# Expert 0's rows gathered by TensorE with a one-hot matrix, the other experts' rows by DMA

## The chip, the cores and the metric

The kernel runs on one core of a Trainium2 chip. The metric is the device time of one launch in microseconds, lower is better. The core has a matrix engine (TensorE, PE in the rows), VectorE (DVE), ScalarE (ACT), GpSimd (POOL) and SyncE (SP), an on-chip memory of 128 partitions (SBUF), the matmul output memory of eight banks (PSUM), and 16 DMA engines to the memory off chip (DRAM).

## The reference, cut to what matters

One decoder layer over 512 tokens of width 1024: input projections, block-sparse attention and a gated recurrence, an output projection and a layer norm. The result of this norm, x1, goes through a mixture of 16 experts, two for each token, and a second norm:

```
x = layer_norm(DEEPNORM_ALPHA * x + mix, ln1_g[l], ln1_b[l])          # x1
g_w, g_idx = lax.top_k(softmax(xt @ w_group + b_group), 1)            # one group of four
e_w, e_idx = lax.top_k(e_prob, EXPERT_TOPK)                           # two experts in it
for e in range(N_EXPERTS):
    h = jax.nn.silu(xt @ w_gate[e]) * (xt @ w_up[e])
    y = y + combine[:, e:e + 1] * (h @ w_down[e])
x = layer_norm(DEEPNORM_ALPHA * x + moe, ln2_g[l], ln2_b[l])
```

## The kernel before

The kernel is written out for each engine, with semaphores between them. No planner orders the work: each engine runs its own list from top to bottom.

Products in float32 are done in three passes. A matrix is split into a high part, which ScalarE copies in a rounded form (`hi`, `ehi`, `xt_hi`), and a low part, which VectorE gets by subtraction (`lo`, `elo`, `xt_lo`). The helper `three` (lines 537 to 541) then issues three matmuls. Weights come in units of 1 MB, which SP loads into a ring of 12 slots. The split writes them into 3 working buffers, and TensorE multiplies from there.

After the output projection x1 lies in SBUF as `x_res`, token by token, in ring slots 9 and 10; the norm's weights are in slot 11. SP writes x1 to DRAM (line 384), and TensorE transposes it for the router's logits. VectorE chooses the experts (lines 1472 to 1511). TensorE counts the tokens ahead of each token in its expert, and VectorE makes from this `r_at1`, each token's place in its expert.

For each expert e VectorE's `place(e)` (line 1521) makes a one-hot matrix of 512 tokens by 128 places, and TensorE's `placed(e)` (line 830) multiplies four blocks of it with a record of two columns (token number, output row). The matrices rotate in five buffers. `slots_of` turns the sums into row numbers, for experts 0 and 1 first. With them GpSimd gathers the expert's rows of x1 from DRAM into `xg` (`gather`, line 482), and TensorE transposes them (`transpose_x`, line 842). The high and low parts of the transposed rows are `e_hi` and `e_lo`.

The expert's work is six units: two of the gate, two of up, two of down. Expert 0's gate units are `in_unit(2, 0, ...)` at lines 902 and 903. Its up units come after the places of experts 9 to 15 and after the transposes of expert 1 (lines 904 to 908). From then on `step` runs one expert's gate, the former's down, and the next one's transposes, in a loop. While TensorE waits it issues dummy matmuls (`keep_warm`, line 543), which write to a bank that nobody reads.

Before expert 0, TensorE places experts 0 to 8 (`EARLY = 9`), issues 26 dummies, waits for the gather, transposes, and issues 22 dummies (lines 837 to 901). SP, once x1 is in DRAM, loads units 6 to 11, and then unit n as soon as unit n - 12 is split (lines 385 to 409).

Of the kernel before, what the change touches and what calls it, by code (L numbers as in the profile page):

```python
# [18 lines left out]
F32 = mybir.dt.float32  # L19
# [8 lines left out]
P = 128  # L28
# [14 lines left out]
F_FLOOR = 2.0 ** -63  # L43
EARLY = 9
CAP = 128
# [61 lines left out]
def build(nc, t, out):  # L107
    with ExitStack() as ctx:
# [3 lines left out]
        def sem(name):  # L112
            return ctx.enter_context(nc.semaphore(name))
# [88 lines left out]
        record = act_lo[:, 7, 0:2 * T * NE].rearrange("p (i e r) -> p i e r", i=T, e=NE)  # L202

        def o_off(i):
            return P * (i * (i + 1) // 2)
# [65 lines left out]
        s_prod, s_copied, s_qkhi, s_qklo, s_av = sem("s_prod"), sem("s_copied"), sem("s_qkhi"), sem("s_qklo"), sem("s_av")  # L271
        s_sq, s_ms, s_sqrt, s_r, s_gate = sem("s_sq"), sem("s_ms"), sem("s_sqrt"), sem("s_r"), sem("s_gate")
        s_tab, s_strip, s_stripsb, s_stripd, s_strips = sem("s_tab"), sem("s_strip"), sem("s_stripsb"), sem("s_stripd"), sem("s_strips")
# [7 lines left out]
        s_pads, s_slotw, s_slots = sem("s_pads"), sem("s_slotw"), sem("s_slots")  # L281
        s_out, s_eps, s_x1n, s_rneed, s_memz, s_firsthead = sem("s_out"), sem("s_eps"), sem("s_x1n"), sem("s_rneed"), sem("s_memz"), sem("s_firsthead")
        s_st1, s_st2, s_bn, s_lg, s_res = sem("s_st1"), sem("s_st2"), sem("s_bn"), sem("s_lg"), sem("s_res")
        s_fw, s_facc, s_fl, s_fn, s_fm = sem("s_fw"), sem("s_facc"), sem("s_fl"), sem("s_fn"), sem("s_fm")
        s_xg = sems("s_xg", 2)
        s_et, s_ethi, s_etlo = sem("s_et"), sem("s_ethi"), sem("s_etlo")
        s_silu, s_h, s_ht, s_hthi, s_htlo = sem("s_silu"), sem("s_h"), sem("s_ht"), sem("s_hthi"), sem("s_htlo")
# [4 lines left out]
        s_xo, s_fin, s_fv, s_fs, s_ft = sem("s_xo"), sem("s_fin"), sem("s_fv"), sem("s_fs"), sem("s_ft")  # L292

# [26 lines left out]
        def _(sp):  # L320
# [65 lines left out]
            sp.wait_ge(s_x1t, T)  # L386
            for n in (6, 7, 8):
                expert_unit(step[n - 4], 1, 0, n + 3)
            sp.wait_ge(s_lo, 16)
            expert_unit(step[5], 1, 0, 0)  # L390
            for n in (10, 11):
                sp.wait_ge(s_lo, n + 7)
                expert_unit(step[n - 10], 2, 1, (n + 3) % RING)

            with sp.Fori(0, NE // 2 - 2) as j:
# [44 lines left out]
            for i in range(T - 1):  # L440
                sp.wait_ge(s_fin, i + 1)
                sp.dma_start(out[i * P:(i + 1) * P, :], f_x1[:, i, :]).then_inc(s_out, 16)
# [8 lines left out]
        def _(pool):  # L451
# [78 lines left out]
            for i in range(T - 1):  # L530
                pool.wait_ge(s_fm, i + 1)
                pool.tensor_tensor(f_x1[:, i, :], f_x1[:, i, :], f_b, ALU.add).then_inc(s_fin, 1)

        @block.tensor
        def _(pe):
# [417 lines left out]
        def _(act):  # L954
# [199 lines left out]

            xt_hi(0, 0)
            ehi(3, 0)
            ehi(4, 0)
            silu(0, 2, 0)
            xt_hi(1, 1)
# [29 lines left out]
            for i in range(T):  # L1189
                act.wait_ge(s_fv, i + 1)  # L1190
                act.activation(rstd[:, i:i + 1], mv[:, i, 1:2], ACT.Sqrt, bias=eps_ln).then_inc(s_fs, 1)
                if i == T - 1:
                    continue
                act.wait_ge(s_fl, i + 1)
                act.activation(f_x1[:, i, :], f_x1[:, i, :], ACT.Identity, scale=rstd[:, i:i + 1], bias=nmr[:, i:i + 1]).then_inc(s_fn, 1)

        @block.vector
        def _(dve):
# [44 lines left out]
            dve.memset(misc[:, 0:1024], 0.0).then_inc(s_zero, 1)  # L1244
            dve.memset(flat(10), 0.0).then_inc(s_memz, 1)
            dve.wait_ge(s_stripd, 16)
# [25 lines left out]
            def keep(g):  # L1272

                dve.wait_ge(s_prod, g + 1)
                if g == 0:
                    dve.wait_ge(s_memz, 1)
                mask = cst[:, C_MASK + 64 * (g // 4):C_MASK + 64 * (g // 4) + 64].bitcast(U32)
# [47 lines left out]
            lo(6)  # L1325
            dve.wait_ge(s_zero, 2)
            dve.wait_ge(s_evac, 8)
# [92 lines left out]
            def norm_tail(x, i, g, b, ready, std, pieces=1):  # L1420

                dve.scalar_tensor_tensor(out=x, in0=x, scalar=mv[:, i, 0:1], in1=g, op0=ALU.subtract, op1=ALU.mult).then_inc(s_cent, 1)
                dve.wait_ge(std, i + 1)
                link(dve.reciprocal(rstd[:, i:i + 1], rstd[:, i:i + 1]))
# [15 lines left out]
            for i in range(T + 1):  # L1440
# [20 lines left out]
                if i == T:  # L1461
                    norm_tail(x_res[:, T - 1, :], T - 1, lng, lnb, s_x1last, s_std)
            for i in range(T):
# [117 lines left out]

            xt_lo(0, 0)
            for e in range(EARLY, NE):
                place(e)
# [26 lines left out]
            for i in range(T + 1):  # L1611
# [4 lines left out]
                if 1 <= i < T:  # L1616
                    dve.wait_ge(s_fs, i)
                    shift_scale(i - 1).then_inc(s_fl, 1)
                if i < T:
# [3 lines left out]
                if 1 <= i < T:  # L1623
                    dve.wait_ge(s_fn, i)
                    dve.tensor_tensor(f_x1[:, i - 1, :], f_x1[:, i - 1, :], f_g, ALU.mult).then_inc(s_fm, 1)
                if i < T:
                    dve.wait_ge(s_facc, 2 * i + 2)
                    stats(y, i)
                    dve.wait_ge(s_bn, 2 * (T + i) + 2)
                    dve.bn_aggr(mv[:, i, :], bst[:, i, :, :].rearrange("p b n -> p (b n)")).then_inc(s_fv, 1)  # L1630
                    dve.wait_ge(s_fv, i + 1)
            norm_tail(f_x1[:, T - 1, :], T - 1, f_g, f_b, s_finlast, s_fs, 2)

# [22 lines left out]
```

## Time and profile before

| what | us |
|---|---|
| median of 3 runs | 704.07 (703.86 to 704.9) |
| the profiled execution, its own time | 701.99 |
| its span, first to last instruction | 700.1 |

The profile is of one execution. Times are in us from the start of its span unless ns is written. The kinds of lines:

- A group of instructions gives line, engine, operation, output and inputs, shapes, count, total busy time and the mean in ns. A line of one source gives duration in ns (least, median, most), the first and last start and the form.
- A piece of the chain that ended last gives start, length, engine, what it wrote and its line. "x8" means eight instructions.
- A line of the timeline gives start, length, engine, line, operation and shapes. In brackets stands the idle time before it and what ended that.
- A line of windows gives a stretch, its length, the busy time and number of instructions of PE, PE's weight loads, DVE, ACT and POOL, the clock granted to TensorE (1.00 is 2.4 GHz, 0.50 is 1.2 GHz), the busy share of the DMA engines and GB/s.

### The profile page before, as it was taken

Reading aid. Unit: us, or ns where it says so; the run is one execution under the profiler, and the core shown is the slowest. Engines: PE = TensorE matmul, PEld = TensorE weight load, DVE = VectorE, ACT = ScalarE, POOL = GpSimd, SP = SyncE. Lnnn points to the kernel's source line nnn. Section 1 sums busy time; section 2 is a strip of 40 time slices with the busy share of each in tenths; the row PEclk is TensorE's granted clock in tenths of the full one; section 3 lists DMA queues with packets and bytes.
Section 4 is the critical chain, followed back from the end, with each engine's and each line's share of the span. In section 5 each row is a group of like instructions: output and inputs, shape, how many; then the busy total and the mean of one; then the engine's idle time right before and its main releaser. Section 6 shows DMA issues by size and latency. Waiting matters only on the chain.

```text
span 700.1 us, 10045 instructions
## 1 busy us (share of the span) xinstructions
PE 646.5 (92%) x3900; PEld 524.9 (75%) x3900; DVE 492.5 (70%) x560; ACT 378.7 (54%) x388; POOL 94.8 (14%) x67
## 2 busy tenths in 40 slices
PE   5998999999999999999989999999999999999800
PEld 4877777777767878888878888888888888888600
DVE  4558797884347336139567888888888988898368
ACT  4458334431207665124305877787777777777511
POOL 0003122360000000003143111111111000000112
PEclk9999999999999999999679999999999999999955
DMA  9632221123005001941793999999999999974063
GB/s 340 206 119 72 70 105 61 61 65 121 2 1 181 1 1 46 302 198 61 295 367 122 337 383 398 394 409 382 387 396 405 392 399 389 402 295 177 16 255 120
DMA packets 40159, 152.83 MB, mean 218 GB/s; under 512 B 10835, under 2 KB 11027, under 8 KB 27836
## 3 DMA queue, kind: packets, MB, share of 16 engines
q1 hardware_dynamic: 35132, 139.68, 52.8%
q0 software_dynamic: 4992, 12.66, 4.6%
q8 instruction: 25, 0.41, 0.2%
q14 instruction: 10, 0.08, 0.0%
HBM read 143.84 MB, written 12.68 MB: 224 GB/s over the span
## 4 chain that ended last, share of the span: by engine, by line
PE 83%; DVE 7%; ACT 4%; DMA 2%; issue 2%; POOL 1%; SPq 0%; DVEq 0%; POOLq 0%; ACTq 0%
PE psum L539 22%; PE psum L541 20%; PE psum L540 20%; PE psum L548 4%; PE psum L743 3%; PE psum L624 2%; PE psum L848 2%; PE psum L807 1%; DMA ring<-in_x 1%; PE psum L833 1%; DVE small L1433 1%; PE psum L865 1%; PE psum L721 1%; PE psum L654 1%; PE psum L734 1%
## 5 line engine op out<-in xcount | busy, mean ns | idle before, releaser
L1407 DVE TENSOR_TENSOR w_lo<-ring,w_hi 128x2048 fp32r<-128x2048 f32 x96 | 218.2, 2289 | 42.5 <-ACT w_hi L1094 42.4
L539 PE MATMUL psum<-w_hi,act_hi 128*128 128x512 f32 x544 | 220.1, 405 | 1.9 <-ACT ring L1015 1.9
L541 PE MATMUL psum<-w_hi,act_lo 128*128 128x512 f32 x544 | 212.7, 391 | 0.0
L540 PE MATMUL psum<-w_lo,act_hi 128*128 128x512 f32 x544 | 212.4, 390 | 0.0
L1094 ACT ACTIVATE w_hi<-ring 128x2048 fp32r<-128x2048 f32 x96 | 182.6, 1917 | 46.8 <-PE psum L541 46.8
L539 PEld LDWEIGHTS psum<-w_hi,act_hi 128*128 128x128 f32 x544 | 102.4, 188 | 27.6 <-issue 3.5
L541 PEld LDWEIGHTS psum<-w_hi,act_lo 128*128 128x128 f32 x544 | 102.1, 188 | 22.0
L540 PEld LDWEIGHTS psum<-w_lo,act_hi 128*128 128x128 f32 x544 | 102.4, 188 | 18.8
L1213 DVE TENSOR_TENSOR w_lo<-ring,w_hi 128x2048 fp32r<-128x2048 f32 x18 | 44.2, 2456 | 43.2 <-ACT w_hi L960 43.0
L960 ACT ACTIVATE w_hi<-ring 128x2048 fp32r<-128x2048 f32 x18 | 34.5, 1916 | 55.4 <-PE psum L541 51.5
L539 PE MATMUL psum<-act_hi,w_hi 128*128 128x512 f32 x128 | 52.0, 406 | 0.2 <-DVE act_lo L1221 0.2
L540 PE MATMUL psum<-act_lo,w_hi 128*128 128x512 f32 x128 | 50.0, 391 | 0.0
L541 PE MATMUL psum<-act_hi,w_lo 128*128 128x512 f32 x128 | 50.0, 391 | 0.0
L506 POOL DMA_INDIRECT pair_dram<-misc,slots x16 | 15.9, 996 | 251.3 <-ACT misc L1138 251.3
L548 PE MATMUL psum<-cst 128*128 128x256 bf16 x286 | 41.6, 309 | 6.2 <-DMA cst<-in_c_main 6.2
L548 PEld LDWEIGHTS psum<-cst 128*128 128x128 bf16 x286 | 31.2, 112 | 13.6 <-DMA cst<-in_c_main 6.2
L1270 DVE TENSOR_TENSOR misc<-ring 64x256 f32<-64x256 f32 x48 | 38.3, 799 | 1.0
L1385 DVE CUSTOM_DVE_ANT_0 ring<-psum,ring 128x128 f32<-128x128 f32 (+3 forms) x32 | 14.4, 488 | 26.9 <-PE psum L721 26.9
L481 POOL TENSOR_TENSOR ring<-ring 128x1024 f32<-128x1024 f32 x3 | 8.0, 2673 | 175.2 <-DVE ring L1460 175.2
L464 POOL TENSOR_TENSOR ring<-ring 128x2048 f32<-128x2048 f32 x6 | 22.2, 3696 | 62.9 <-PE psum L624 51.9
L539 PEld LDWEIGHTS psum<-act_hi,w_hi 128*128 128x128 f32 x128 | 24.0, 188 | 6.5 <-issue 1.2
L541 PEld LDWEIGHTS psum<-act_hi,w_lo 128*128 128x128 f32 x128 | 24.0, 188 | 5.2
(199 smaller groups left out, 728.4 us busy)
## 6 DMA issues: line engine op xcount, KB each, us to landing
ring<-in_w_gate SPq DMA_DIRECT2D x32, 1024.0 KB, 7.5
ring<-in_w_up SPq DMA_DIRECT2D x32, 1024.0 KB, 7.7
ring<-in_w_down SPq DMA_DIRECT2D x32, 1024.0 KB, 7.3
ring<-in_w_in SPq DMA_DIRECT2D x14, 1024.0 KB, 5.6
ring<-in_x SPq DMA_DIRECT2D x2, 2048.0 KB, 8.8
ring<-in_w_o SPq DMA_DIRECT2D x4, 1024.0 KB, 5.0
ring<-pair_dram SPq DMA_DIRECT2D x8, 512.0 KB, 7.6
ring<-strip_dram SPq DMA_DIRECT2D x8, 256.0 KB, 4.6
```

Source lines behind the costliest of these rows:

```text
L464: pool.tensor_tensor(wlev[l].rearrange("p a (n s) -> p (a n) s", s=2 * m), src, src[:, :, m - 1:m].broadcast_to((P, SEQ * PAIRS // (2 * m) ...
L506: pool.indirect_dma_start(out=pair_dram, out_offset=bass.IndirectOffsetOnAxis(ap=slots[:, e, 1:2].bitcast(U32), axis=0), in_=yb[:, e % 2, ...
L539: pe.matmul(dst, lh, rh, start=first, stop=False, skip_group_check=True)
L540: pe.matmul(dst, lh, rl, start=False, stop=False, skip_group_check=True)
L541: return pe.matmul(dst, ll, rh, start=False, stop=last, skip_group_check=True)
L548: pe.matmul(psum[:, b, 0:2 * P], half[:, 0:P], half, start=True, stop=True, skip_group_check=True)
L743: last = pe.matmul(psum[:, i, h * DH:(h + 1) * DH], pt_buf(h, i)[:, j * P:(j + 1) * P], av[:, j, h * DH:(h + 1) * DH], start=(j == 0), sto ...
L960: act.activation(w_hi[:, u % WBUF, :], ring[:, u % MIX_RING, :], ACT.Copy).then_inc(s_hi, 1)
L1094: act.activation(w_hi[:, v0 % WBUF, :], ring[:, slot, :], ACT.Copy).then_inc(s_hi, 1)
L1213: dve.tensor_tensor(w_lo[:, u % WBUF, :], ring[:, u % MIX_RING, :], w_hi[:, u % WBUF, :].bitcast(F32), ALU.subtract).then_inc(s_lo, 1)
L1270: dve.tensor_tensor(qz[rows, a, :, par, :].rearrange("p c (n t) -> p c n t", t=m), right(wlev[l]), right(hq), ALU.mult).then_inc(s_qz, 1)
L1407: dve.tensor_tensor(w_lo[:, v0 % WBUF, :], ring[:, slot, :], w_hi[:, v0 % WBUF, :].bitcast(F32), ALU.subtract).then_inc(s_lo, 1)
```

## The change

Expert 0's rows no longer go through DRAM. TensorE multiplies `x_res`, eight slices of 128 columns, each over four blocks of tokens, with expert 0's one-hot matrix (`first_rows`). The product is expert 0's block of x1, already transposed, in PSUM banks 0 and 1. It is copied and split in two halves, the first with semaphores of its own (`s_half`, `s_halfhi`, `s_halflo`), and unit 0 waits for the first half only. `gather(0)`, the transposes of expert 0 and 48 dummy matmuls go. Experts 0 and 1 are placed after the first two slices, 2 to 4 after the eighth, and 5 to 15 after expert 0's gate units. The matrix of expert 0 keeps a buffer of its own, the others rotate in four (`hot_of`). VectorE does `elo(2, 0)` after the address and weight chain and after the splits of expert 0's rows, and the two operations on the counts after `place(1)`. Since `first_rows` reads `x_res` in slots 9 and 10, SP loads units 6 and 7 only when it is done (`s_et`), after units 8 to 11. The rest of the diff merges semaphores (`s_fin`, `s_fv`, `s_fs`, `s_fl`, `s_fn`, `s_fm` into those of the first norm, `s_memz` into `s_zero`) with counts raised to fit.

```diff
@@ -201,6 +200,9 @@
         one_hot = [act_hi[:, 5, :], act_hi[:, 6, :], act_hi[:, 7, :], act_lo[:, 5, :], act_lo[:, 6, :]]
         record = act_lo[:, 7, 0:2 * T * NE].rearrange("p (i e r) -> p i e r", i=T, e=NE)
 
+        def hot_of(e):
+            return 0 if e == 0 else 1 + (e - 1) % 4
+
         def o_off(i):
             return P * (i * (i + 1) // 2)
 
...
@@ -384,13 +387,15 @@
                 sp.dma_start(x1_dram[i * P:(i + 1) * P, :], x_res[:, i, :]).then_inc(s_x1out, 16)
             sp.wait_ge(s_x1out, 16 * T)
             sp.wait_ge(s_x1t, T)
-            for n in (6, 7, 8):
-                expert_unit(step[n - 4], 1, 0, n + 3)
+            expert_unit(step[4], 1, 0, 11)
             sp.wait_ge(s_lo, 16)
             expert_unit(step[5], 1, 0, 0)
             for n in (10, 11):
                 sp.wait_ge(s_lo, n + 7)
                 expert_unit(step[n - 10], 2, 1, (n + 3) % RING)
+            sp.wait_ge(s_et, 1)
+            for n in (6, 7):
+                expert_unit(step[n - 4], 1, 0, n + 3)
 
             with sp.Fori(0, NE // 2 - 2) as j:
                 for q in range(12):
...
@@ -481,14 +486,13 @@
                 pool.tensor_tensor(x_res[:, i, :], x_res[:, i, :], lnb, ALU.add).then_inc(s_x1, 1)
             def gather(e):
 
-                if e >= 2:
+                if e >= 3:
                     pool.wait_ge(s_et, e - 1)
                 pool.indirect_dma_start(out=xg[:, e % 2, :], out_offset=None, in_=x1_dram,
                                         in_offset=bass.IndirectOffsetOnAxis(ap=slots[:, e, 0:1].bitcast(U32), axis=0)).then_inc(s_xg[e % 2], 16)
 
             pool.wait_ge(s_slots, 1)
             pool.wait_ge(s_x1out, 16 * T)
-            gather(0)
             gather(1)
 
             pool.wait_ge(s_pads, 16 * (SEQ // P))
...
@@ -830,20 +834,36 @@
             def placed(e):
                 pe.wait_ge(s_onehot, e + 1)
                 for i in range(T):
-                    last = pe.matmul(psum[:, 7 if e < 2 else 6, 2 * e:2 * e + 2], one_hot[e % 5][:, i * P:(i + 1) * P], record[:, i, e, :],
+                    last = pe.matmul(psum[:, 5 if e < 2 else 6, 2 * e:2 * e + 2], one_hot[hot_of(e)][:, i * P:(i + 1) * P], record[:, i, e, :],
                                      start=(i == 0), stop=(i == T - 1), skip_group_check=True)
                 last.then_inc(s_placed, 1)
 
-            for e in range(EARLY):
+            def first_rows(k):
+
+                for i in range(T):
+                    last = pe.matmul(psum[:, k // 4, (k % 4) * P:(k % 4 + 1) * P], x_res[:, i, k::KD],
+                                     one_hot[0][:, i * P:(i + 1) * P].bitcast(F32), start=(i == 0), stop=(i == T - 1), skip_group_check=True)
+                return last
+
+            pe.wait_ge(s_onehot, 1)
+            for k in range(2):
+                first_rows(k)
+            for e in range(2):
                 placed(e)
-            keep_warm(26, 1)
-
-
-            def transpose_x(e, b, first=False):
-
-                pe.wait_ge(s_xg[b], 8 * (e - b) + 16)
-                if not first:
-                    pe.wait_ge(s_etlo, e)
+            for k in range(2, 4):
+                last = first_rows(k)
+            last.then_inc(s_half, 1)
+            for k in range(4, KD):
+                last = first_rows(k)
+            last.then_inc(s_et, 1)
+            for e in range(2, 5):
+                placed(e)
+
+
+            def transpose_x(e, b):
+
+                pe.wait_ge(s_xg[b], 8 * (e - b) + 16 * b)
+                pe.wait_ge(s_etlo, e)
                 for k in range(KD):
                     last = pe.transpose(psum[:, k // 4, (k % 4) * P:(k % 4 + 1) * P], xg[:, b, k::KD], ident)
                 last.then_inc(s_et, 1)
...
@@ -896,12 +916,11 @@
                 in_unit(3, b, 0, v + 4, j)
                 in_unit(3, b, 1, v + 5, j)
 
-            transpose_x(0, 0, first=True)
-            keep_warm(22, 4)
+            pe.wait_ge(s_halflo, 1)
+            in_unit(2, 0, 0, 0, 0)
             pe.wait_ge(s_etlo, 1)
-            in_unit(2, 0, 0, 0, 0)
             in_unit(2, 0, 1, 1, 0)
-            for e in range(EARLY, NE):
+            for e in range(5, NE):
                 placed(e)
             transpose_x(1, 1)
             in_unit(3, 0, 0, 2, 0)
...
@@ -1152,9 +1171,13 @@
                 if ahead:
                     ehi(v + 8, j)
 
-            xt_hi(0, 0)
+            act.wait_ge(s_half, 1)
+            act.activation(e_hi[:, 0, 0:512], bank(0), ACT.Copy).then_inc(s_halfhi, 1)
+            act.wait_ge(s_et, 1)
+            act.activation(e_hi[:, 0, 512:D], bank(1), ACT.Copy).then_inc(s_ethi, 1)
             ehi(3, 0)
             ehi(4, 0)
+            act.wait_ge(s_flag, 2)
             silu(0, 2, 0)
             xt_hi(1, 1)
             ehi(5, 0)
...
@@ -1521,9 +1544,9 @@
             def place(e):
 
                 if e >= 5:
-                    dve.wait_ge(s_placed, e - 4)
+                    dve.wait_ge(s_placed, e - 3)
                 slot_no = cst[:, C_SLOT:C_SLOT + CAP].rearrange("p (a n) -> p a n", a=1).broadcast_to((P, T, CAP))
-                dve.tensor_tensor(one_hot[e % 5].rearrange("p (i n) -> p i n", i=T), slot_no, r_at1[:, :, e:e + 1].broadcast_to((P, T, CAP)),
+                dve.tensor_tensor(one_hot[hot_of(e)].rearrange("p (i n) -> p i n", i=T), slot_no, r_at1[:, :, e:e + 1].broadcast_to((P, T, CAP)),
                                   ALU.is_equal).then_inc(s_onehot, 1)
 
             def slots_of(e0, e1, bank_no):
...
@@ -1532,15 +1555,14 @@
                 dve.tensor_tensor(slots[:, e0:e1, :].rearrange("p e r -> p (e r)"), psum[:, bank_no, 2 * e0:2 * e1],
                                   cst[:, C_PAD + 2 * e0:C_PAD + 2 * e1], ALU.add).then_inc(s_slots, 1)
 
+            for e in range(2):
+                place(e)
             link(dve.tensor_reduce(r_cnt, psum[:, 7, T * NE:(T + 1) * NE], AX.X, ALU.max))
             link(dve.tensor_scalar(r_pos, pos, float(NE), None, ALU.mult))
-            for e in range(2):
+            place(2)
+            slots_of(0, 2, 5)
+            for e in range(3, 5):
                 place(e)
-            place(2)
-            slots_of(0, 2, 7)
-            for e in range(3, EARLY):
-                place(e)
-            elo(2, 0)
             link(dve.tensor_tensor(r_pos, r_pos, bc(e16, NE), ALU.add))
             for k in range(2):
                 link(dve.tensor_tensor(r_t16, r_pos, r_sel[:, k], ALU.mult))
...
@@ -1553,6 +1575,11 @@
             link(dve.tensor_tensor(wgt[:, :, 1:2], r_gw, r_top2, ALU.mult))
             link(dve.tensor_scalar(r_cnt, r_cnt, float(CAP), None, ALU.is_gt))
             dve.tensor_copy(over_i[:, :], r_cnt).then_inc(s_flag, 1)
+            dve.wait_ge(s_halfhi, 1)
+            dve.tensor_tensor(e_lo[:, 0, 0:512], bank(0), e_hi[:, 0, 0:512].bitcast(F32), ALU.subtract).then_inc(s_halflo, 1)
+            dve.wait_ge(s_ethi, 1)
+            dve.tensor_tensor(e_lo[:, 0, 512:D], bank(1), e_hi[:, 0, 512:D].bitcast(F32), ALU.subtract).then_inc(s_etlo, 1)
+            elo(2, 0)
 
             def xt_lo(e, b):
                 dve.wait_ge(s_ethi, e + 1)
...
@@ -1579,8 +1606,7 @@
                 if ahead:
                     elo(v + 8, j)
 
-            xt_lo(0, 0)
-            for e in range(EARLY, NE):
+            for e in range(5, NE):
                 place(e)
             elo(3, 0)
             slots_of(2, NE, 6)
```

## Rows read from the trace of the kernel before

**Rows 1.** The page, parts 1 and 6.

```profile
PE 646.5 (92%) x3900; PEld 524.9 (75%) x3900; DVE 492.5 (70%) x560; ACT 378.7 (54%) x388; POOL 94.8 (14%) x67
...
ring<-in_w_down SPq DMA_DIRECT2D x32, 1024.0 KB, 7.3
```

**Rows 2.** Windows, one step of the expert loop.

```profile
486.00:504.00 18.00, 18.00 (x86) 14.82 (x85) 15.96 (x10) 14.20 (x11) 1.98 (x2) 1.00 1.01 390
```

**Rows 3.** The chain that ended last, 350 to 379 us.

```profile
350.85 0.24 DVE misc L1518
...
354.38 5.03 PE psum L833 x24
359.41 5.60 PE psum L548 x26
365.01 0.96 PE psum L848 x8
...
368.37 0.47 PE psum L539
...
374.12 3.02 PE psum L833 x28
377.13 1.02 PE psum L848 x8
378.15 0.23 PE psum L539
```

**Rows 4.** One source, line 486: GpSimd's gathers and their landing.

```profile
L486 POOL DMA_INDIRECT misc<-x_dram,slots x16: 980/980/2784, 354.0 to 613.6; - x16
...
DMA to landing us min/median/max: 8.7/9.8/11.5
```

**Rows 5.** Timeline, VectorE and ScalarE, 351 to 387 us.

```profile
351.58 1.90 DVE L1526 TENSOR_TENSOR act_hi<-cst,misc 128x512 fp32r<-128x512 f32 x3
...
357.26 2.28 DVE L1407 TENSOR_TENSOR w_lo<-ring,w_hi 128x2048 fp32r<-128x2048 f32 x1
...
359.46 0.22 DVE L1544 TENSOR_TENSOR misc<-misc,cst 128x64 f32<-128x64 f32 x1
...
361.99 0.15 DVE L1555 CAST over_i<-misc 128x1 int32<-128x1 f32 x1
...
383.72 1.92 ACT L1094 ACTIVATE w_hi<-ring 128x2048 fp32r<-128x2048 f32 x1 [0.80 <-PE psum L541]
...
385.16 0.68 DVE L1565 TENSOR_TENSOR misc<-psum,misc 128x512 f32<-128x512 f32 x1
...
386.86 0.60 ACT L1131 ACTIVATE act_hi<-psum 128x512 fp32r<-128x512 f32 x1 [1.22 <-PE psum L865]
```

**Rows 6.** Groups by line and form, TensorE.

```profile
L743 PE MATMUL psum<-ring 128*128 128x64 f32 x160 | 21.2, 279 | 0.7 <-ACT ring L1071 0.7
```

**Rows 7.** The chain again, two earlier stretches.

```profile
206.34 1.02 PE psum L654 x8
...
257.62 1.93 PE psum L743 x16
```

**Rows 8.** Windows, stretches of small and of larger matmuls.

```profile
354.90:359.30 4.40, 4.40 (x22) 4.38 (x23) 4.40 (x6) 0.00 (x0) 1.76 (x2) 0.50 1.01 422
...
373.70:377.00 3.30, 3.30 (x31) 3.23 (x29) 2.51 (x3) 2.77 (x2) 0.00 (x0) 1.00 0.00 0
...
337.80:341.20 3.40, 3.40 (x32) 3.33 (x30) 0.18 (x1) 2.69 (x3) 0.00 (x0) 0.99 0.58 167
341.40:347.90 6.50, 6.50 (x32) 4.94 (x33) 3.98 (x23) 2.15 (x3) 0.00 (x0) 0.50 1.00 416
...
335.20:337.60 2.40, 2.40 (x13) 2.40 (x14) 0.77 (x3) 0.44 (x1) 0.00 (x0) 0.50 0.86 350
```

**Rows 9.** Timeline, SP's queue, 338 to 379 us.

```profile
338.66 0.81 SPq L364 DMA_DIRECT2D ring<-in_w_down  x2
...
359.74 18.75 SPq L364 DMA_DIRECT2D ring<-in_w_up  x2
```

More of the change, by code:

```diff
@@ L43 @@
 F_FLOOR = 2.0 ** -63
-EARLY = 9
 CAP = 128
@@ L271, in build @@
         s_prod, s_copied, s_qkhi, s_qklo, s_av = sem("s_prod"), sem("s_copied"), sem("s_qkhi"), sem("s_qklo"), sem("s_av")
-        s_sq, s_ms, s_sqrt, s_r, s_gate = sem("s_sq"), sem("s_ms"), sem("s_sqrt"), sem("s_r"), sem("s_gate")
+        s_sq, s_ms, s_sqrt, s_gate = sem("s_sq"), sem("s_ms"), sem("s_sqrt"), sem("s_gate")
         s_tab, s_strip, s_stripsb, s_stripd, s_strips = sem("s_tab"), sem("s_strip"), sem("s_stripsb"), sem("s_stripd"), sem("s_strips")
@@ L281, in build @@
         s_pads, s_slotw, s_slots = sem("s_pads"), sem("s_slotw"), sem("s_slots")
-        s_out, s_eps, s_x1n, s_rneed, s_memz, s_firsthead = sem("s_out"), sem("s_eps"), sem("s_x1n"), sem("s_rneed"), sem("s_memz"), sem("s_firsthead")
+        s_out, s_eps, s_x1n, s_rneed, s_firsthead = sem("s_out"), sem("s_eps"), sem("s_x1n"), sem("s_rneed"), sem("s_firsthead")
         s_st1, s_st2, s_bn, s_lg, s_res = sem("s_st1"), sem("s_st2"), sem("s_bn"), sem("s_lg"), sem("s_res")
-        s_fw, s_facc, s_fl, s_fn, s_fm = sem("s_fw"), sem("s_facc"), sem("s_fl"), sem("s_fn"), sem("s_fm")
+        s_fw, s_facc = sem("s_fw"), sem("s_facc")
         s_xg = sems("s_xg", 2)
         s_et, s_ethi, s_etlo = sem("s_et"), sem("s_ethi"), sem("s_etlo")
+        s_half, s_halfhi, s_halflo = sem("s_half"), sem("s_halfhi"), sem("s_halflo")
         s_silu, s_h, s_ht, s_hthi, s_htlo = sem("s_silu"), sem("s_h"), sem("s_ht"), sem("s_hthi"), sem("s_htlo")
@@ L291, in build @@
         s_pairs = sems("s_pairs", 2 * T)
-        s_xo, s_fin, s_fv, s_fs, s_ft = sem("s_xo"), sem("s_fin"), sem("s_fv"), sem("s_fs"), sem("s_ft")
+        s_xo, s_ft = sem("s_xo"), sem("s_ft")
         w_in = t["w_in"].rearrange("(p k) (b n) -> p k b n", p=P, n=WIDTH)
@@ L440, in _ @@
             for i in range(T - 1):
-                sp.wait_ge(s_fin, i + 1)
+                sp.wait_ge(s_x1, T - 1 + i + 1)
                 sp.dma_start(out[i * P:(i + 1) * P, :], f_x1[:, i, :]).then_inc(s_out, 16)
@@ L530, in _ @@
             for i in range(T - 1):
-                pool.wait_ge(s_fm, i + 1)
-                pool.tensor_tensor(f_x1[:, i, :], f_x1[:, i, :], f_b, ALU.add).then_inc(s_fin, 1)
+                pool.wait_ge(s_lg, T - 1 + i + 1)
+                pool.tensor_tensor(f_x1[:, i, :], f_x1[:, i, :], f_b, ALU.add).then_inc(s_x1, 1)
         @block.tensor
@@ L1189, in _ @@
             for i in range(T):
-                act.wait_ge(s_fv, i + 1)
-                act.activation(rstd[:, i:i + 1], mv[:, i, 1:2], ACT.Sqrt, bias=eps_ln).then_inc(s_fs, 1)
+                act.wait_ge(s_var, T + i + 1)
+                act.activation(rstd[:, i:i + 1], mv[:, i, 1:2], ACT.Sqrt, bias=eps_ln).then_inc(s_std, 1)
                 if i == T - 1:
                     continue
-                act.wait_ge(s_fl, i + 1)
-                act.activation(f_x1[:, i, :], f_x1[:, i, :], ACT.Identity, scale=rstd[:, i:i + 1], bias=nmr[:, i:i + 1]).then_inc(s_fn, 1)
+                act.wait_ge(s_ln, T - 1 + i + 1)
+                act.activation(f_x1[:, i, :], f_x1[:, i, :], ACT.Identity, scale=rstd[:, i:i + 1], bias=nmr[:, i:i + 1]).then_inc(s_x1n, 1)
         @block.vector
@@ L1244, in _ @@
             dve.memset(misc[:, 0:1024], 0.0).then_inc(s_zero, 1)
-            dve.memset(flat(10), 0.0).then_inc(s_memz, 1)
+            dve.memset(flat(10), 0.0).then_inc(s_zero, 1)
             dve.wait_ge(s_stripd, 16)
@@ L1275, in keep @@
                 if g == 0:
-                    dve.wait_ge(s_memz, 1)
+                    dve.wait_ge(s_zero, 2)
                 mask = cst[:, C_MASK + 64 * (g // 4):C_MASK + 64 * (g // 4) + 64].bitcast(U32)
@@ L1325, in _ @@
             lo(6)
-            dve.wait_ge(s_zero, 2)
+            dve.wait_ge(s_zero, 3)
             dve.wait_ge(s_evac, 8)
@@ L1422, in norm_tail @@
                 dve.scalar_tensor_tensor(out=x, in0=x, scalar=mv[:, i, 0:1], in1=g, op0=ALU.subtract, op1=ALU.mult).then_inc(s_cent, 1)
-                dve.wait_ge(std, i + 1)
+                dve.wait_ge(s_std, std)
                 link(dve.reciprocal(rstd[:, i:i + 1], rstd[:, i:i + 1]))
@@ L1461, in _ @@
                 if i == T:
-                    norm_tail(x_res[:, T - 1, :], T - 1, lng, lnb, s_x1last, s_std)
+                    norm_tail(x_res[:, T - 1, :], T - 1, lng, lnb, s_x1last, T)
             for i in range(T):
@@ L1616, in _ @@
                 if 1 <= i < T:
-                    dve.wait_ge(s_fs, i)
-                    shift_scale(i - 1).then_inc(s_fl, 1)
+                    dve.wait_ge(s_std, T + i)
+                    shift_scale(i - 1).then_inc(s_ln, 1)
                 if i < T:
@@ L1623, in _ @@
                 if 1 <= i < T:
-                    dve.wait_ge(s_fn, i)
-                    dve.tensor_tensor(f_x1[:, i - 1, :], f_x1[:, i - 1, :], f_g, ALU.mult).then_inc(s_fm, 1)
+                    dve.wait_ge(s_x1n, T - 1 + i)
+                    dve.tensor_tensor(f_x1[:, i - 1, :], f_x1[:, i - 1, :], f_g, ALU.mult).then_inc(s_lg, 1)
                 if i < T:
@@ L1629, in _ @@
                     dve.wait_ge(s_bn, 2 * (T + i) + 2)
-                    dve.bn_aggr(mv[:, i, :], bst[:, i, :, :].rearrange("p b n -> p (b n)")).then_inc(s_fv, 1)
-                    dve.wait_ge(s_fv, i + 1)
-            norm_tail(f_x1[:, T - 1, :], T - 1, f_g, f_b, s_finlast, s_fs, 2)
+                    dve.bn_aggr(mv[:, i, :], bst[:, i, :, :].rearrange("p b n -> p (b n)")).then_inc(s_var, 1)
+                    dve.wait_ge(s_var, T + i + 1)
+            norm_tail(f_x1[:, T - 1, :], T - 1, f_g, f_b, s_finlast, 2 * T, 2)
 SHAPES = {
```

## The prediction, made before the change was run

> **What bounds the kernel now.** I read the page first: TensorE is busy 92% of the span [rows 1]. The reader should then ask at which stage it is really the limit. In the middle of the expert loop one step takes 18.0 us. TensorE is busy for all of it at full clock, while VectorE and ScalarE have 2.0 and 3.8 us to spare, and the DMA engines move 390 GB/s [rows 2]. So from the third expert on nothing but TensorE's own work counts. Whatever makes expert 0 start earlier reaches the end of the span unchanged, as long as the weights come along.
>
> The chain in order of time, between the routing and expert 0 [rows 3], shows where TensorE works for nothing. The router's positions are ready at 350.85. VectorE needs until about 352.3 for the first one-hot matrix [rows 5]. TensorE places 9 experts until 359.4 and then issues 26 and, after the transposes of expert 0 at 365.0, another 22 dummy matmuls. The real work starts at 368.37. The transposes wait for the gather of expert 0. It was issued at 354.0, and gathers take 8.7 us at least to land [rows 4]. That is the wait which the change takes away.
>
> **What takes its place.** Expert 0's transposed rows now need only the one-hot matrix and x1, which has long been in SBUF.
>
> VectorE: the two small operations on the counts move behind two place operations, so place(0) starts at 351.1, 0.47 us earlier [rows 3, 5]. Three places take 1.90 us [rows 5], 0.63 each, so TensorE may start at 351.9.
>
> TensorE: 32 f32 matmuls, 128x128 by 128 columns. None like them stands in the trace except transposes. An ordinary f32 matmul appears as two records: L743 has 160 for 80 matmuls [rows 6]. Of such halves 16 with 64 columns take 1.93 us (0.121 each), and 8 with 128 columns but a narrower weight take 1.02 (0.128) [rows 7]. Transposes of the full shape, one record each, take 1.02 for 8, 0.128 [rows 3]. So I take 0.125 for each of 64 halves, 8.0 us. The lower bound is the 0.108 of the two-column matmuls, which do little but load weights (28 in 3.02 [rows 3]), or 6.9 us. The upper one is load and stream one after the other, twice 0.108, or 13.8 us. I take the value near the nearest rows. With them go placed(0) to placed(4), 20 matmuls at 0.108, 2.2 us. First_rows(0,1) end at 353.9, placed(0,1) at 354.8, first_rows(2,3) at 356.8, the other four at 360.8 and placed(2..4) at 362.1.
>
> The copies: a half takes ScalarE 0.60 us and VectorE's subtraction 0.68 [rows 5]. VectorE gets to the first only after place(3), place(4) (to 356.3) and the address and weight chain, 2.7 us long (359.46 to 362.14 [rows 5]). So s_halflo comes at 359.7 and is hidden behind first_rows. The second half is done at 362.2, while unit 0 runs. The elo(2) that stood before the chain, 2.28 us [rows 5], now comes behind these two and runs 362.2 to 364.5, for a unit needed at 374. Without that cover it would cost its 2.3 us.
>
> Unit 0 of expert 0 so starts at 362.1 instead of 368.4: 6.3 us earlier. Units 0 and 1 take 5.75 us, as before (368.37 to 374.12 [rows 3]), until 367.85.
>
> **What is given back.** Only 5 experts are placed early instead of 9, so 11 instead of 7 are placed after unit 1. On TensorE the four more cost 16 x 0.108 = 1.7 us. But expert 0's matrix keeps its buffer, so only four rotate. VectorE can prepare 5 to 8 from 364.5 to 367.0, and 9 has to wait for placed(5), until 368.3. From there seven places at 0.62 go to 372.7, and the last placed ends at 373.3. VectorE paces this stretch: 5.4 us against 3.0. Transposes of expert 1 then go to 374.3, and unit 2 starts there instead of at 378.15 [rows 3]. That is 3.9 us gained, if the clock holds.
>
> **The clock.** The windows say that it will not. From 337.8 to 341.2 TensorE was busy 3.40 of 3.40 us, with 20-column matmuls (L807), at 0.99. From 341.4 to 347.9 the grant was 0.50, though 256-column matmuls were running for nearly all of it. The nine placed experts, two columns each, ended at half clock too, 0.50 from 354.9 to 359.3. The seven of the second stretch, with real work close on both sides, kept 1.00 [rows 8]. The new stretch is 5.4 us of the same two-column matmuls. If the clock falls 3 us into it, and stays down 6.5 us, as from 341.4 to 347.9, it is at 1.2 GHz from 370.9 to 377.4. The last four placed then take 0.21 a matmul (24 in 5.03 us [rows 3]) and the stretch ends at 374.1, 0.8 later. The 3.3 us left at half clock do 1.65 us of work. Together 2.5 us are lost, which leaves 3.9 - 2.5 = 1.4 us.
>
> The Trainium skill ("TensorE: Matmul & The Clock Gate", section "Why this matters for your kernels") says that the clock stays up if the engine is kept busy and has no idle gaps. By that rule the stretch would cost no clock and 3.9 us would be the gain. The trace disagrees: the 3.40 busy us just named were followed by 0.50.
>
> **Edits that I cost at nothing.** SP: after x1 is written only units 8 to 11 are issued. Units 6 and 7, whose slots hold x1, now wait for s_et at 360.8, and units 12 onward are queued behind them. Before, eight units left from 338.7 on, and the next at 359.7 [rows 9]. Unit 6 is first read by ehi(6), at 383.72 before [rows 5], now 379 or later. At 7.3 us to land [rows 1] it has 11 us of cover. If that failed, each late us would be a us of the span. Units 12 onward are needed an expert later still. POOL: gather(0) is gone. Gather(1) is issued at about 355.3, lands by 367 at the longest landing, 11.5 us [rows 4], and is needed at 373.3. The eight slot_dram scatters behind it wait for the addresses, which come 3 us sooner. ScalarE: the wait on s_flag before the first silu is met at 359, ten us early. PSUM bank 5, the merged semaphores and the waits of the last norm are the same work as before: nothing.
>
> **From the profile to the runs.** The profiled execution took 701.99 us, its span of 700.1 and 1.9 around it. The median of the runs is 704.07, 2.1 above. I subtract the gain from the median. All three timed runs lie 1.9 to 2.9 us above the profiled one. A clock that fell in the old stretch of seven as well would do that, and then the new stretch would not be charged for it in the comparison. I cannot show it, and add 0.5 us for it: gain 1.9 us, 702.2 us, for this case a range of 700.6 to 703.3.
>
> **Rivals.**
> 1. The clock holds in the stretch of 11, because unit 1 before it and the transposes behind it count for enough, as they did for the stretch of seven. Against it: the new stretch is 2.4 us longer and has no other matmul in it. Gain 3.9: 700.2 us.
> 2. The other side: the clock falls already under first_rows. TensorE idles for the 1.1 us before it, and two placed experts follow after 2.0 us. If the 16 halves between do not hold it, 6.5 us from about 354 on run at half and lose 3.3, and the later fall still comes: 1.4 - 3.3 = -1.9, 706.0 us. It decides from 2.8 us at half clock on, since those cost the 1.4 us of gain. For it: in the old kernel the clock was down by 354.9 after nearly the same idle time. Against it: there only two-column matmuls followed, here they have 128 columns, and the 128-column transposes from 335.2 to 337.6 brought it back to 0.99 [rows 8].
> 3. The f32 matmuls with full weight and full width cost 0.2 a half, near the upper bound: 4.8 us more, 1.4 - 4.8 = -3.4, 707.5 us. Against it is that transposes of the full shape take 0.128 [rows 3].
> 4. The start is earlier but another wait sets it: units 6 and 7 too late, or the subtraction on VectorE, or the time is lost in the expert loop. Then nothing is left: 704.1 us. The cover of 11 us speaks against it.
>
> **Chances.** Forecast 0.50, rival 1 0.17, rival 2 0.13, rival 3 0.06, rival 4 0.14. The measurement can tell about 0.2%, 1.4 us. Faster by more than that: rival 1 and 0.42 of the forecast, 0.59. Slower: rival 3 and 0.08 of rival 2, 0.14. Within: 0.27. The range reaches from a little below rival 1 (699.6) to just under rival 2 (705.6).
>
> **What would show it.** Unit 0's first L539 matmul at 362 and not 368. The matmuls of first_rows in 8 us and not 14. Placed of 5 to 15 in 5 to 6 us. A granted clock of 0.5 somewhere in 370 to 378 and back at 1.0 after it. Unit 2 at 375 to 376. ScalarE's w_hi copies never waiting on a DMA. The forecast is wrong if the clock is down before 360, if it holds through 378, or if steps of the expert loop are not 18.0 us any more.

## The result and the profile after

The changed kernel is slower: 711.09 us, median of 5 runs (709.48 to 713.7), against 704.04 (702.72 to 704.9). That is 7.05 us, a ratio of 1.0100 (1.0079 to 1.0121). The forecast was 702.2.

Rival 3 is what happened: the f32 matmuls of `first_rows` cost twice what I had taken. The profiled execution took 711.5 us, its span is 709.7. Here is its chain of waits in order of time (start, length, what; L844 is `first_rows`, L837 `placed`, L868 the transposes, L543 the first matmul of a triple). It answers to [rows 3].

```profile
354.08 0.23 DVE misc L1541
...
355.18 4.04 PE psum L844 x16
359.22 0.79 PE psum L837 x8
360.01 11.55 PE psum L844 x48
...
372.79 0.34 PE psum L543
...
378.38 6.14 PE psum L837 x44
384.52 1.83 PE psum L868 x8
386.35 0.43 PE psum L543
...
388.91 0.28 PE psum L543
```

Between the router's positions and unit 0 now lie 18.7 us (354.08 to 372.79), where there were 17.5 (350.85 to 368.37). The forecast was 11.2 (350.85 to 362.1). The 64 halves (an f32 matmul makes two records, and each is called a half here) take 4.04 + 11.55 = 15.59 us, 0.244 each. The rows of that source, and below them those of `placed`, say which part of a half is slow:

```profile
L844 PEld LDWEIGHTS psum<-act_hi,ring x64: 313/336/338, 355.2 to 371.0; 128*128 128x128 f32 x64
...
L837 PEld LDWEIGHTS psum<-act_lo,act_hi x36: 186/192/338, 358.9 to 383.2; 128*128 128x128 f32 x36
```

The weight load takes 336 ns in the median. The weight loads of the few-column matmuls, with as many f32 columns but side by side, took 192. The windows of the changed kernel (the last three numbers are clock, DMA share and GB/s) show two more things:

```profile
362.00:365.00 3.00, 3.00 (x14) 3.00 (x14) 2.02 (x12) 0.60 (x1) 1.09 (x2) 0.50 0.57 175
365.00:371.00 6.00, 6.00 (x27) 6.00 (x26) 0.39 (x1) 0.00 (x0) 4.77 (x5) 1.00 0.02 1
...
378.40:381.90 3.50, 3.50 (x31) 3.43 (x31) 3.14 (x6) 3.39 (x3) 0.00 (x0) 1.00 0.98 360
382.10:384.40 2.30, 2.30 (x13) 2.30 (x12) 2.30 (x3) 0.20 (x1) 0.00 (x0) 0.50 1.02 431
```

From 362 to 365 the clock was at 1.2 GHz and `first_rows` went on at the pace that it had at 2.4 GHz: 14 in 3 us and 27 in 6, where each count takes in those that reach over an edge. In the trace the starts of its records lie 0.240 us apart at 1.2 GHz and 0.238 at 2.4. So TensorE's clock does not set its pace. And the late stretch went as forecast: the clock fell 3.7 us into it and came back at 388.9.

Where the 9.6 us between the two spans went, piece by piece:

| piece | before | after | more |
|---|---|---|---|
| until the router's positions | 350.85 | 354.08 | +3.2 |
| positions to unit 0 | 17.52 | 18.71 | +1.2 |
| units 0 and 1 | 5.75 | 5.59 | -0.2 |
| late places | 3.02 | 6.14 | +3.1 |
| transposes of expert 1 | 1.02 | 1.83 | +0.8 |
| six matmuls of unit 2 at half clock, 0.43 for 0.23 | | | +1.2 |

This makes 9.3 of 9.6. No edit stands behind the first line: TensorE's instructions up to there are the same. In the chain of the changed kernel the router's last two groups of transposes and logits (L805, L811) took

```profile
335.59 3.49 PE psum L805 x16
339.08 6.65 PE psum L811 x32
```

where before they took 3.01 and 4.28. Before, the clock was back at 337.7 [rows 8]; here it stayed at 0.50 until 351.4. Of the nine profiled executions with the same instructions in that place (the two kernels and experiments 1 to 6 and 9), four had 3.6 to 4.3 us for the second and five 6.65 or 6.66. The three that derive from the kernel before are all short, and of the six that derive from the changed one five are long and one is short. The kernels of experiments 2 and 5 are the same up to that place, and one is short and the other long. So it varies from execution to execution without any edit, and whether the change makes the long form more frequent stays open. Without that line the pieces come to 6.1 us, and the medians are 7.05 apart (5.6 to 8.5 by the ratio).

### The profile page after: what moved, and what is told of

Same layout as the page of the kernel before. It is cut to its first block, busy times and chain, and to the rows that moved or that the text cites. A ratio compares the mean times of both kernels' runs of the same rounds, so it can differ in the third digit from the quotient of the medians.

```text
span 709.7 us, 10069 instructions
## 1 busy us (share of the span) xinstructions
PE 656.7 (93%) x3908; PEld 536.7 (76%) x3908; DVE 492.9 (69%) x561; ACT 379.0 (53%) x389; POOL 92.8 (13%) x66
## 4 chain that ended last, share of the span: by engine, by line
PE 84%; DVE 7%; ACT 4%; DMA 2%; issue 2%; POOL 1%; SPq 0%; DVEq 0%; POOLq 0%; ACTq 0%
PE psum L543 22%; PE psum L545 20%; PE psum L544 20%; PE psum L552 3%; PE psum L747 3%; PE psum L844 2%; PE psum L628 2%; PE psum L868 2%; PE psum L811 2%; DMA ring<-in_x 1%; DVE small L1456 1%; PE psum L885 1%; PE psum L837 1%; PE psum L725 1%; PE psum L658 1%
## 5 line engine op out<-in xcount | busy, mean ns | idle before, releaser
L543 PE MATMUL psum<-w_hi,act_hi 128*128 128x512 f32 x544 | 220.7, 406 | 1.9 <-ACT ring L1034 1.9
L543 PEld LDWEIGHTS psum<-w_hi,act_hi 128*128 128x128 f32 x544 | 102.8, 189 | 27.5 <-issue 3.5
L543 PE MATMUL psum<-act_hi,w_hi 128*128 128x512 f32 x128 | 51.9, 406 | 0.2 <-DVE act_lo L1244 0.2
L552 PE MATMUL psum<-cst 128*128 128x256 bf16 x238 | 33.5, 301 | 6.1 <-DMA cst<-in_c_main 6.1
L552 PEld LDWEIGHTS psum<-cst 128*128 128x128 bf16 x238 | 25.4, 110 | 11.8 <-DMA cst<-in_c_main 6.1
L543 PEld LDWEIGHTS psum<-act_hi,w_hi 128*128 128x128 f32 x128 | 24.0, 187 | 6.5 <-issue 1.2
```

What stands on the lines that cost most here:

```text
L543: pe.matmul(dst, lh, rh, start=first, stop=False, skip_group_check=True)
L552: pe.matmul(psum[:, b, 0:2 * P], half[:, 0:P], half, start=True, stop=True, skip_group_check=True)
```

## The experiments

Beside the variants the kernel before took 702.8 us in the median, both times that it was run with them. That is 1.2 below the 704.04 above, so variants are compared by their ratio to it: 1.0100 for the changed kernel.

**1. The disputed cost by itself.** The kernel before, with 40 dummies and eleven groups of 8 matmuls where it had 26 dummies:

```diff
-            keep_warm(26, 1)
+            keep_warm(40, 1)
+            src = cst[:, 0:D]
+            hot3 = one_hot[3].bitcast(F32)
+            dst = psum[:, 1, 0:P]
+            for q in range(8):
+                pe.matmul(dst, src[:, 0:P], ident, start=True, stop=True, skip_group_check=True)
...
+            for q in range(8):
+                pe.matmul(dst, src[:, q::KD], ident, start=True, stop=True, skip_group_check=True)
...
```

> The kernel before, with the 26 dummies in front of expert 0's transposes replaced by 40 dummies and eleven groups of 8 matmuls of 128 columns, which write to a bank that nobody reads; only its trace counts, not its time. In the changed kernel each half of a first_rows matmul took 0.24 us, at full and at half clock alike, where I had 0.125. Stride theory: the weights are read with a step of 8 elements (32 bytes), and this read sets the pace: groups with contiguous weights take 0.12 to 0.13 a half whatever the moving operand, groups with a step of 8 take 0.24, and steps of 2 and 4 lie at or between these. Width theory: an f32 half with 128 weight columns and 128 moving columns takes 0.24 by itself, load and stream one after the other: then contiguous groups take 0.24 too. Moving theory: the one-hot operand is what is slow: then only the groups with it take 0.24.

Its chain, one group a row (16 halves where an f32 matmul makes two records). L844 has contiguous weights, L846, L848 and L850 weights with a step of 2, 4 and 8 elements. L852 and L854 have the one-hot matrix as moving operand, with a step of 8 and contiguous weights. L856 has contiguous weights and a moving step of 8. L858 and L860 are transposes with a step of 8 and contiguous, L862 and L864 f32r matmuls, contiguous and with a weight step of 4:

```profile
365.42 1.79 PE psum L844 x16
367.20 1.88 PE psum L846 x16
369.08 3.73 PE psum L848 x16
372.82 3.81 PE psum L850 x16
376.63 3.81 PE psum L852 x16
380.44 1.79 PE psum L854 x16
382.22 3.73 PE psum L856 x16
385.95 0.89 PE psum L858 x8
386.84 0.87 PE psum L860 x8
387.71 0.85 PE psum L862 x8
388.56 1.86 PE psum L864 x8
```

The clock was at full level for all of them:

```profile
365.40:390.40 25.00, 25.00 (x147) 24.57 (x146) 0.00 (x0) 0.00 (x0) 4.85 (x5) 1.00 0.04 11
```

Contiguous weights take 1.79 / 16 = 0.112 a half, a step of 2 takes 0.117, a step of 4 takes 0.233 and of 8 0.238. The one-hot operand makes no difference (L852 against L850, L854 against L844). Width theory and moving theory fall. The f32r matmul behaves the same (L862 contiguous 0.106, L864 with a step of 4 0.233). Not foreseen: a moving operand with a step of 8 is as slow (L856, 0.233), and a transpose is not slowed at all (L858, 0.111, against 0.109 contiguous, L860). This is why the transposes, which read x1 with just that step, misled me. Why they are not slowed, no run shows.

**2. Contiguous weights in the changed kernel.**

```diff
-    last = pe.matmul(psum[:, k // 4, (k % 4) * P:(k % 4 + 1) * P], x_res[:, i, k::KD],
+    last = pe.matmul(psum[:, k // 4, (k % 4) * P:(k % 4 + 1) * P], x_res[:, i, k * P:(k + 1) * P],
...
+            def first_unit(m, slot):
+
+                src = t["w_gate" if m[0] == "g" else "w_up"][0].rearrange("(k p) f -> p k f", p=P)
+                sp.dma_start(ring[:, slot, :].rearrange("p (k f) -> p k f", k=4), src[:, 4 * m[1]:4 * m[1] + 4, :]).then_inc(s_raw[slot], 16)
...
-                expert_unit(m, n // 4, 0, (n + 3) % RING)
+                if n < 4:
+                    first_unit(m, n + 3)
+                else:
+                    expert_unit(m, n // 4, 0, (n + 3) % RING)
```

> The changed kernel with contiguous weights in first_rows: slice k is columns 128k to 128k+127 of x1 instead of every eighth column, and expert 0's four gate and up units are loaded in the matching row order, so the result is the same. Stride theory: 64 halves go from 0.24 to 0.12 or 0.13, 15.6 us to about 8, all on the path: 7 to 7.5 us less than the changed kernel, 711.1 to about 704. Width theory: nothing changes, 711 us.

702.67 us against 702.78, ratio 0.9991 (0.9974 to 1.0009), from 1.0100. By the ratios 7.7 us are back (5.7 to 9.6). In the trace the way from the positions to unit 0 is 6.5 us shorter, 12.2 us (351.88 to 364.12) for 18.7. Its chain (L852 is `first_rows`, L845 `placed`, L876 the transposes):

```profile
352.98 3.29 PE psum L852 x16
...
357.42 5.46 PE psum L852 x48
...
364.12 0.35 PE psum L551
...
369.73 5.93 PE psum L845 x44
375.65 1.83 PE psum L876 x8
377.48 0.43 PE psum L551
```

The last 48 halves take 5.46 us, 0.114 each, where they took 11.55. The first 16 take 3.29. The clock fell at 353.5 in this execution and was back at 356.9, so rival 2, which the slow reads had hidden, is real as well: it costs 1.5 us in these 16, and 0.4 in the two places behind them. With contiguous weights the kernel only breaks even, because the late stretch still gives back what the start gains.

**3. Dummies in the late stretch.**

```diff
             for e in range(5, NE):
                 placed(e)
+                keep_warm(2, 4)
```

> The changed kernel with two dummy matmuls of 256 columns after each of placed(5) to placed(15). Clock theory (the fall at 382 in the changed kernel comes from eleven experts of two-column matmuls in a row): the clock stays at 1.0 from 372 to 390. The dummies cost 22 x 0.11 = 2.4 us, of which VectorE's pace already hides some, and what the half clock took (0.8 in the transposes, 1.3 in unit 2, 0.8 in the last places) comes back: 710 to 711 us and a clock of 1.0. Rival (the grant follows something else): the clock falls all the same and the kernel is 1 to 2 us slower, 712 to 713 us.

712.22 us, ratio 1.0131 (1.0109 to 1.0152), in four runs. The clock held in the profiled one, as its windows show:

```profile
377.00:385.50 8.50, 8.50 (x80) 8.21 (x79) 7.26 (x11) 4.13 (x4) 0.20 (x1) 1.00 1.01 421
385.50:390.00 4.50, 4.50 (x22) 3.69 (x21) 2.86 (x2) 2.66 (x2) 2.58 (x1) 1.00 0.93 324
```

The time did not follow. The stretch and the transposes took 7.5 us (6.6 and 0.9) instead of 8.0, and unit 2 ran at full clock, which makes 1.7 us in the profile. The median shows none of it: the profiled execution, 709.23 us, was the fastest of the four, and by the ratios the version is 2.2 us slower than the changed kernel, with intervals that overlap. That the run of few-column matmuls brings the clock down is shown by all the profiled executions together: where the eleven places stand in one piece (the changed kernel, experiments 2 and 7) the clock fell within them, three times of three, and where other matmuls stand between them (experiments 3 to 6 and 8) it never did, in five. That dummies are a cheap cure is not shown.

**4. The late places spread.**

```diff
             in_unit(2, 0, 0, 0, 0)
+            for e in range(5, 9):
+                placed(e)
             pe.wait_ge(s_etlo, 1)
             in_unit(2, 0, 1, 1, 0)
-            for e in range(5, NE):
+            for e in range(9, 13):
                 placed(e)
             transpose_x(1, 1)
             in_unit(3, 0, 0, 2, 0)
+            for e in range(13, NE):
+                placed(e)
```

On VectorE `place(5)` to `place(8)` go before `elo(2, 0)`, and `slots_of(2, NE, 6)` behind `xt_lo(1, 1)`.

> The changed kernel with the eleven late experts spread: 5 to 8 placed between expert 0's two gate units, 9 to 12 after them, 13 to 15 after the first up unit, VectorE's places in step, slots_of behind the split of expert 1's rows. Clock and pacing theory: VectorE's pace (6.1 us for the eleven instead of 4.8) and the fall of the clock (2.1 us behind the stretch) both go: 3 to 3.5 us less, 707.6 to 708. Rival (the stretch is late only because first_rows is): within 1 us of 711.

708.23 us, ratio 1.0067 (1.0047 to 1.0087). Its chain:

```profile
377.18 1.68 PE psum L837 x16
...
381.74 1.68 PE psum L837 x16
383.42 1.02 PE psum L868 x8
...
387.19 1.23 PE psum L837 x12
```

The eleven experts take 1.68 + 1.68 + 1.23 = 4.6 us, the bare 0.105 a matmul, instead of 6.14. The clock is at 1.00 throughout and the transposes take 1.02. From the start of `first_rows` to unit 2 the trace is 3.5 us shorter than the changed kernel's, when the three places that now follow are counted in and so are the 1.2 us of the half-clock matmuls. The ratios give 2.3 us (0.3 to 4.4), less than the 3 to 3.5 foreseen and clear of zero.

**5. Both.**

> Contiguous weights in first_rows and the late places spread, together. If the two causes are separate they add: contiguous weights took the changed kernel from 711.1 to 702.7, spreading from 711.1 to 708.2. Additive theory: 702.7 - 2.9 = 699.8 us, below the kernel before by about 3 us. Rival (both act through the same clock stretches, or VectorE becomes the limit when TensorE is early): 701.5 to 702.7 us.

699.86 us, ratio 0.9943 (0.9917 to 0.9970). The two ratios before it would give 1.0100 - 0.0109 - 0.0033 = 0.9958. They add, as far as the interval can tell: the causes are separate, and the version beats the kernel before. Its first 16 halves were slow again, with the clock down from 356.3 to 359.8:

```profile
356.21 3.65 PE psum L852 x16
```

**6. Both, and dummies in the gap.**

```diff
+            keep_warm(9, 4)
             pe.wait_ge(s_onehot, 1)
```

> The last kernel with 9 dummy matmuls (1.0 us) while TensorE waits for the first one-hot matrix. With contiguous weights the clock fell at 353.6, 0.6 us into first_rows, and its first 16 halves took 3.29 us where the others had 0.114 each, 1.8 us. If the idle time and the few-column matmuls before it brought the fall, the dummies hold the clock there: 1.5 us less, 698.3. Rival (the fall comes from the whole stretch and not from the gap, or falls in few runs only): within 0.5 us of the last kernel.

696.91 us, ratio 0.9912 (0.9884 to 0.9939). Its chain:

```profile
354.63 2.05 PE psum L852 x16
...
364.17 0.35 PE psum L551
```

The first 16 halves take 2.05 us, where the kernel of experiment 5 had 3.65; the clock was at full level. From the start of `first_rows` to unit 0 are 9.5 us; the forecast had 10.2. The ratios give the dummies 2.2 us, give or take 2.7, so their own share is not settled. The fall before, in two executions of two (experiments 2 and 5), and its absence here agree with the theory; experiment 8, which has the same nine dummies, does not.

**7 and 8. The router.**

```diff
                 logits(i)
+                if i == 0:
+                    keep_warm(8, 1)
                 logits(i + 1)
+                if i == 0:
+                    keep_warm(8, 1)
```

> The changed kernel with 8 dummies before and after the second logits group of the router, where TensorE waits for the last rows of x1 anyway. It asks how much of the difference between the two profiled executions, before and after, is the router's clock: there 32 pairs of 20-column matmuls took 6.65 us in the one and 4.28 in the other with no edit between them. Theory (the clock is at half in that stage in some runs and not in others): the router's end, the first one-hot matrix, comes 2 to 3 us earlier than the 354.3 of the changed kernel, 708 to 709 us with a narrower spread. Rival (it falls again within the logits): 711 us.

> All four edits: contiguous weights, spread places, dummies in the gap, dummies in the router. If they add: 699.8 - 1.5 - 2.5 = 695.8 us. If the clock edits do not hold: 699 to 700 us.

Experiment 7, on the changed kernel: 712.44 us, ratio 1.0117 (1.0086 to 1.0148), a miss. The clock fell at 331.6, as the first logits ended and before the first of the new dummies could help, and the second logits took 3.23 us where the first had 1.70. Experiment 8, with all edits: 698.81, ratio 0.9937 (0.9913 to 0.9962), no better than experiment 6. In its profiled execution, 696.08 us, the fastest of six, the router's clock did hold, at 0.98 from 330 to 350; in the medians nothing is left of it. But here the clock fell at 349.2, in the midst of the nine dummies of experiment 6, and the first 16 halves ran at half clock for the most part (a window, and below it a piece of the chain):

```profile
349.30:352.60 3.30, 3.30 (x17) 3.01 (x16) 2.21 (x5) 0.00 (x0) 0.00 (x0) 0.50 0.35 149
...
350.28 3.00 PE psum L856 x16
```

So the nine dummies do not keep the clock up in every execution: of the two profiled with them, one fell. How often the clock falls in the router, and on what that depends, stays open.

**9. Which steps are slow.** The edit is that of experiment 1 with other operands, for example

```diff
+            for q in range(8):
+                pe.matmul(dst, src[:, 0:3 * P:3], ident, start=True, stop=True, skip_group_check=True)
```

The groups: f32 weights with a step of 3 (L844) and of 2 from an odd start (L846); a moving step of 2 (L848), 3 (L850, not shown) and 4 (L852); a step of 8 on both sides (L854); step 8 with 64 columns (L856) and with 512 (L858), contiguous with 512 (L860); bf16 weights with a step of 4 (L862) and 8 (L864), and contiguous (L866, not shown).

> The kernel before with twelve groups of 8 matmuls in place of the 26 dummies; only its trace counts. The first such run gave 0.112 us a half with contiguous weights, 0.117 with a step of 2 elements and 0.23 to 0.24 with a step of 4 or 8, and 0.233 too when the moving operand had a step of 8. 
```profile
365.15 2.77 PE psum L844 x16
367.93 1.88 PE psum L846 x16
369.81 1.82 PE psum L848 x16
...
374.70 3.63 PE psum L852 x16
378.34 3.79 PE psum L854 x16
382.12 3.65 PE psum L856 x16
385.77 8.74 PE psum L858 x16
394.51 6.87 PE psum L860 x16
401.38 0.45 PE psum L862 x8
401.83 0.50 PE psum L864 x8
```

A step of 3 takes 0.173, between the two levels. By the line theory two of four such reads share a line and two stand alone, which puts it midway between 0.117 and 0.233, at 0.175 (an estimate). A step of 2 takes 0.117 from an odd start too. A moving step of 2 is free (0.114), one of 3 lies between (3.02 us, 0.19) and one of 4 is not free (0.227). Both sides slow cost no more than one (0.237). 64 columns do not help (0.228).

With 512 columns the chain seems to say that the slow weight load is not hidden, 8.74 us against 6.87. But the clock fell under the first of the two groups (two windows, and below them the group's weight loads from 389.6 on):

```profile
386.00:389.20 3.20, 3.20 (x5) 1.23 (x5) 0.00 (x0) 0.00 (x0) 0.00 (x0) 0.50 0.02 5
389.40:394.50 5.10, 5.10 (x13) 3.50 (x13) 0.00 (x0) 0.00 (x0) 0.00 (x0) 1.00 0.00 0
...
L858 PEld LDWEIGHTS psum<-cst x10: 312/314/314, 389.6 to 393.5; 128*128 128x128 f32 x10
```

The ten weight loads behind the fall start from 389.63 to 393.50, 0.43 us apart, just as in the contiguous group at full clock (6.87 / 16 = 0.429). Within the fall the halves are 0.853 apart. So the slow load does hide behind 512 columns, as expected, and the whole difference is the clock.

One expectation missed: bf16 weights with a step of 16 bytes are hardly slowed (0.063 against 0.056). For f32 matmuls the line theory holds at every step tried; for bf16, and for the transposes of experiment 1, the cause stays open.

## Why the prediction was wrong

The prediction names two ranges, 700.6 to 703.3 and, with the chances, 699.6 to 705.6. 711.09 lies outside both, and the time moved the other way.

- **The bound and what starts the expert loop: right.** A step of the loop, from one expert's transposes to the next one's, is 18.0 us after as before, no wait for SP's late units 6 and 7 (issued at 371.6) shows in the trace, and what was lost up to the first matmuls of unit 2 accounts for 9.3 of the 9.6 us at the end.
- **The failed step: "So I take 0.125 for each of 64 halves, 8.0 us".** It measured 0.244, 15.6 us, beyond even my upper bound of 13.8. I had matched rows by shape and left out the step between the weights' columns. With f32 weights 32 bytes apart the read takes 0.24 a half, at either clock. The only rows with that step that I used were transposes, and these are not slowed. Experiments 1 and 2 show it: the same kernel with contiguous weights has 0.114 and is 7.7 us faster by the ratios. A rule would have warned me. The Trainium skill ("SBUF — State Buffer", section "Door 1: The DMA port swizzle") says that SBUF is read in lines of 16 bytes and that at least two reads must fall in a line for full rate. Steps of 2, 3, 4 and 8 at 0.117, 0.173, 0.233 and 0.238 agree with it; its remark that f32 may step by 4 for free does not agree with them, and the transposes with a step of 8 at 0.111 do not fit the rule.
- **Rival 3, at 0.06, was priced 707.5 with 0.2 a half.** With 0.244 the same sum gives 1.4 - 7.6 = -6.2, 710.3 us, beside 711.1 measured; the pieces of the profile without the router's line, 6.1 us, say the same. The mechanism of the rest held; its chance did not. I let the transposes speak against it twice.
- **The late stretch: right.** Forecast 5.4 us, or 6.2 with the clock falling in it; measured 6.14, the fall 3.7 us in, where I had 3, and the clock back after 6.8 us, where I had 6.5. VectorE's pace was there too: its last one-hot matrix was ready at 383.07, 4.7 us into the stretch, so with the clock held some 5.1 us would have been left (an estimate). Experiment 4 takes both away and wins 2.3 us.
- **Rival 2 (the clock falls under `first_rows`): right as a mechanism.** It fell in the changed kernel only from 361.6 to 365, without cost because the read set the pace. In experiments 2 and 5 it fell at the start, as I had it, but for 3.4 us and not 6.5, and cost 1.8 us, not 3.3.
- **The 0.5 us for a fall in the old stretch of seven: not shown.** The executions differ in the router instead, by up to 3 us in that one stage, and I had not looked there.

## What to carry to other kernels

Before taking a matmul's cost from another row, compare the steps of its operands too, and trust no transpose as a stand-in for a matmul. Lay the data out so that f32 weights and moving columns are side by side; here it cost only another row order in four weight loads. A long run of few-column matmuls (eleven experts' places here) brings the clock down for the work behind it: put them between real matmuls. Before a slow group in a microbenchmark is put down to its operands, look at the clock of its stretch.

## What the runs showed of the hardware

- An f32 matmul of 128 by 128 by 128 takes two records of 0.112 us with contiguous operands and of 0.23 to 0.24 with a step of 4 or 8 elements on either side, and a transpose with a step of 8 takes one of 0.111 (experiments 1 and 9).
- The slow read is at the same pace at 1.2 and 2.4 GHz (0.240 and 0.238 us a record in the changed kernel), where contiguous operands go from 0.213 to 0.112 (experiment 2). It hides behind 512 moving columns (0.43 a record with a step of 8 and without, experiment 9).
- A TensorE busy without a gap, with matmuls of 2 columns, was brought from 1.00 to 0.50 within 3.7 us and held there for 6.8, the last 2.5 of them in 512-column matmuls. The clock also fell within 128-column f32 matmuls, at 361.6 in the changed kernel, while 25 us of such groups in experiment 1 kept 1.00; what decides that stays open.
